# Hybrid decoder trunk: the first quarter of the modulation in two eighths, part of it multiplied by TensorE, and four pieces of the input projection on the first eighth

## The chip, the cores and the metric

The kernel runs on one core of a Trainium2 chip. The metric is the device time of one execution in microseconds (us). Engines: PE = TensorE (matmul; PEld is its weight load), DVE = VectorE, ACT = ScalarE, POOL = GpSimd, SP = SyncE, whose queue issues almost every DMA.

## The reference

Two layers on x of 256 x 2048, all in float32. Each layer first needs its modulation:

```
c_act = silu(c)                                   # 2048
mod = c_act @ ada_w[layer] + ada_b[layer]         # 2048 x 12288 weights per layer
sh_m, sc_m, g_m, sh_f, sc_f, g_f = split(mod, 6)
h = rmsnorm(x, norm_mix[layer]) * (1 + sc_m) + sh_m
mix = attention and gated unit (layer 0) or short convolution (layer 1) of h @ w_in
x = x + g_m * mix
h = rmsnorm(x, norm_ffn[layer]) * (1 + sc_f) + sh_f
x = x + g_f * swiglu(h, ...)
```

w_in of layer 0 is 2048 x 5632: queries, keys, values and the two inputs of the gating unit, 11 groups of 512 columns. Nothing of h exists until the shift (sh_m) and the scale (sc_m) of its features do, so the first matmul of the projection depends on the modulation weights.

## The kernel before, in words

All weights are streamed once from HBM. A piece is 256 rows (two k-tiles of 128) x 512 columns, 512 KB; SP loads it into one of eight `raw` slots, ACT rounds it to its high part `whi` (six slots), DVE subtracts to get the low part `wlo` (in place), and PE multiplies: for each k-tile and each of the two token tiles t three matmuls of 512 columns (high x high, high x low, low x high; L1419 to L1421), 12 matmuls a piece. Two pieces are a unit. `lo_piece`/`hi_piece` work two units ahead of PE (`hi_next`, `lo_next`).

The modulation is a product of one row and a matrix. It is done by DVE: `ada_op(a)` takes one slot of `ada` (128 rows of one k-tile x 1024 columns, 512 KB, six slots) and adds it, times a column of `cact`, to `acc` (L989, L993). After 16 such ops a tile of 1024 columns is summed over k-tiles but not over partitions; `reduce_cols` has PE do that with a moving operand of one column of ones (L1474), eight calls, and `keep_cols` and `quarter_gain` on DVE give `mod` and `gsc`. The tile for the first quarter holds the shift and the scale of features 0 to 511. The order of the modulation tiles is `ADA`, the pace of the ops behind the front is `ADA_PACE`.

The first quarter of h is two tiles (t = 0, 1) of four blocks of 128 features. ACT normalises x (`norm_xn`), PE turns it (`norm_turn`, L1511), ACT scales and shifts it (`norm_scaled`, L669), rounds the high part (`norm_front` for blocks 0 and 1, L680, `norm_back` for blocks 2 and 3, L690), DVE subtracts for the low part (L1055).

The input projection visits its groups by quarters of the features (`VISITS`): first all 11 groups with the first quarter (units 0 to 10), then eight of them with the second, and so on. What a visit leaves in PSUM is evicted by ACT into `kept` (L623); a later visit of the same group begins with ACT writing it back into PSUM (`seed`, L629). PSUM has two accumulators per token tile, used in turn (`acc_bank`), so visit v can begin only when visit v-2 is evicted.

The order of every engine is written out by hand. In the front, PE's program is: idle matmuls on ones (`idle_work`, L1496) paced by DVE's ops 7 to 10 and 12 to 14, a turn, `reduce_cols(0)`, a turn, four idle matmuls, and then the units. SP's program is the column of c, six modulation loads, x, ten modulation loads, four pieces, and then per unit two pieces and the modulation loads of its pace. A modulation load waits until DVE has used the op that had its slot (`summed`). DRAM holds the weights as the reference has them, so that a piece has rows of 2 KB.

Of the kernel before, what the change touches and what calls it, by code (L numbers as in the profile page):

```python
# [14 lines left out]
P = 128  # L15
D = 2048
# [37 lines left out]
VISITS = ([(c, (0,)) for c in IN_ORDER]  # L54
          + [(c, (k,)) for k in (1, 2, 3) for c in IN_ORDER[:EARLY]]
          + [(c, (1, 2, 3)) for c in IN_ORDER[EARLY:]])
IN_UNITS = [(v, c, k) for v, (c, ks) in enumerate(VISITS) for k in ks]
LAST = {c: v for v, (c, ks) in enumerate(VISITS)}
UNIT_OF = {v: max(u for u, x in enumerate(IN_UNITS) if x[0] == v) for v in range(len(VISITS))}
VISIT_AT = {u: v for v, u in UNIT_OF.items()}  # L60
BEFORE = {v: w for v, (c, ks) in enumerate(VISITS) for w in range(v) if VISITS[w][0] == c}

SEEDED = [v for v in BEFORE if len(VISITS[v][1]) == 1]
KEPT = {c: n for n, c in enumerate((0, 3, 1, 4, 2, 5, 9, 10))}
FIRST_OF = {k: min(u for u, x in enumerate(IN_UNITS) if x[2] == k) for k in range(4)}
# [9 lines left out]
GROUP_UNITS = ([len(ks) for c, ks in VISITS] + 4 * [4] + len(F_UNITS) * [1] + (12 - 2 * F_VISITED) * [4] + 4 * [6]  # L75
# [5 lines left out]
GROUP_END = [sum(GROUP_UNITS[:g + 1]) - 1 for g in range(len(GROUP_UNITS))]  # L81
# [8 lines left out]
CLOSING = {2 * u + 1: g for g, u in enumerate(GROUP_END)}  # L90
# [32 lines left out]
ADA = ([(0, SH_M, q) for q in range(4)] + [(0, G_M, n) for n in range(2)]  # L123
       + [(0, SH_F, q) for q in range(4)] + [(0, G_F, n) for n in range(2)]
       + [(1, w, n) for w in (SC_M, SH_M, SC_F, G_M, SH_F, G_F) for n in range(2)])
QUARTERS = 4
QUARTER_OF = {j: (k, q) for k, w in ((0, SH_M), (1, SH_F)) for q in range(4) for j in (ADA.index((0, w, q)),)}
GATES = ((0, G_M), (0, G_F), (1, G_M), (1, G_F))

OPS = [(j, k) for j in range(len(ADA)) for k in range(KT)]  # L130

ANGLES_AT, TRIG_AT = 3, 5
REDUCE_AT = {9: 1, 17: 2, 25: 3}

# [24 lines left out]
def norm_gain(k, q):  # L159
    return 8 + 2 * (k - 2) + q // 2 + 1 if k > 1 else 4 * k + q + 1  # L160
# [29 lines left out]
for j in range(QUARTERS, len(ADA)):  # L190
    u = next(u for u in range(U_END) if ada_to(u) > OPS.index((j, KT - 1))) + 2
    free = [v for v in range(u, U_END) if v - 4 not in SCORE_UNIT and v not in BOUNDARY and not (is_row(j) and v - 4 in BOUNDARY)]
    ADA_REDUCE[j] = tuple(free[:halves(j)])
# [27 lines left out]
for _k in range(4):  # L221
    for _i in range(8):
        BY_SA[_k, _i] = max(BY_SA.values(), default=0) + (2 if (_k, _i) in SHARED else 4)

# [38 lines left out]
def decoder_kernel(nc, x_in, c_col, pos, ada_w, ada_b, g_mix, g_ffn, w_in, sgu_w, sgu_b, w_out,  # L263
                   conv_in, conv_w, conv_out, ff_gate, ff_up, ff_down, g_fin, freq_in, ident_in,
                   mask_in, out):
    with ExitStack() as ctx:
# [94 lines left out]
        ada_step, ada_init, red_done, mod_done, row_done = sems("ada_step ada_init red_done mod_done row_done")  # L361
# [27 lines left out]
        def summed(engine, a):  # L389

            j, k = OPS[a]
            engine.wait_ge(ada_step, KT * j + k + 1)

        def scaled(engine, k, i, blocks=4):
# [5 lines left out]
            else:  # L400
                engine.wait_ge(hf_ready, BY_SA[k, i] - 4 + blocks)
# [9 lines left out]
        def columns_of(v, j):  # L411

            layer, which, n = ADA[j]
            return v[:, :].rearrange("p (w f) -> p w f", f=KT)[:, which:which + 2, 4 * n:4 * n + 4]
# [27 lines left out]
        def rows(w):  # L442
            return w.rearrange("(t p) n -> p t n", p=P)

        def layer_rows(w):
            return w.rearrange("l (t p) n -> l p t n", p=P)

        ada_v, gate_v, up_v, down_v = (layer_rows(w) for w in (ada_w, ff_gate, ff_up, ff_down))
        w_in_v, w_out_v, conv_in_v, conv_out_v = (rows(w) for w in (w_in, w_out, conv_in, conv_out))

        def piece_of(v, k, n):
            return v[:, 2 * k:2 * k + 2, COLS * n:COLS * n + COLS]
# [7 lines left out]
        def feed_pieces(layer):  # L460
            if layer == 0:
                for k, c, w in F_UNITS:
                    for half in range(2):
                        yield piece_of((gate_v, up_v)[w][layer], 2 * k + half, c)
            for half in HALVES:
                for c in half:
                    if visited(layer, c):
                        continue
                    for v, k in in_turn((gate_v, up_v), layer and c == 0):
                        for p in range(2):  # L470
                            yield piece_of(v[layer], 2 * k + p, c)
                for n in range(4):
                    for k in range(2 * half[0], 2 * half[-1] + 2):
                        yield piece_of(down_v[layer], k, n)

        def weight_pieces():

            for v, c, k in IN_UNITS:
                for half in range(2):
                    yield piece_of(w_in_v, 2 * k + half, c)  # L480
            for n, k in OUT_UNITS:
                for half in range(2):
                    yield piece_of(w_out_v, 2 * k + half, n)
            yield from feed_pieces(0)
            for i in range(4):
                for n, k in in_turn((4 + i, 8 + i), i == 0) + [(i, k) for k in range(4)]:
                    for half in range(2):
                        yield piece_of(conv_in_v, 2 * k + half, n)
            for n in range(4):
                for k in range(8):  # L490
                    yield piece_of(conv_out_v, k, n)
# [6 lines left out]
        def _(sp):  # L498
# [7 lines left out]
            def load_ada(a):  # L506
                j, k = OPS[a]
                layer, which, n = ADA[j]
                if a >= ADA_SLOTS:
                    summed(sp, a - ADA_SLOTS)  # L510
                to, w = ada[:, a % ADA_SLOTS], ada_v[layer, :, k, :]
                if j in QUARTER_OF:
                    to = to.rearrange("p (w n) -> p w n", w=2)
                    src = w.rearrange("p (w n) -> p w n", w=6)[:, which:which + 2, COLS * n:COLS * n + COLS]
                else:
                    col = D * which + ADA_COLS * n
                    src = w[:, col:col + ADA_COLS]
                sp.dma_start(to, src).then_inc(ada_loaded[a % ADA_SLOTS], 16)
# [1276 lines left out]
```

## Time and profile before

| | before |
|---|---|
| time, median of 3 runs | 2264.3 us (2264.23 to 2264.5) |
| the profiled execution | 2265.22 us, span 2263.5 us |
| PE busy | 2226.7 us, 98% |
| DVE busy | 1625.4 us, 72% |
| ACT busy | 1154.2 us, 51% |
| DMA queue of SP | 613.5 MB, 80.8% of 16 engines' span |

Busy time is what an engine spent in instructions; the span runs from the first to the last instruction. Times in rows are microseconds from the start of the span. The granted clock is TensorE's, 1.00 for 2.4 GHz and 0.50 for 1.2 GHz.

### The profile page before, as it was taken

To read this page: it belongs to the slowest core of one execution; us is meant where nothing else is said; L and a number is where in the kernel's file an instruction comes from. 1 tells how busy PE (TensorE), PEld (TensorE's weight loads), DVE (VectorE), ACT (ScalarE), POOL (GpSimd) and SP (SyncE) were. 2 spreads that over 40 slices of the span, in tenths; PEclk is the share of its full clock that TensorE was granted. 3 is DMA by queue.
4 is the path that set the end of the run, shared out by engine and by line. 5 is a ranking of instruction groups with operands and counts; after the bars stand their busy time and mean duration, and the time that the engine had idled before them with its cause. 6 is when DMAs were issued, how large, how long until landed. Compare 5 with 4: busy or idle time off the path is not lost.

```text
span 2263.5 us, 26805 instructions
## 1 busy us (share of the span) xinstructions
PE 2226.7 (98%) x10133; PEld 1845.0 (82%) x10133; DVE 1625.4 (72%) x1644; ACT 1154.2 (51%) x1541; POOL 102.6 (5%) x71
## 2 busy tenths in 40 slices
PE   5999999999999999999999999999999999999998
PEld 3888888888888888888888888888888888888887
DVE  6888899788887767777778877887664454545455
ACT  4688774687544344444474444446444433344443
POOL 0003201000000100000100000010000010000010
PEclk9999999999999999999999999999999999999999
DMA  9999889899888888888878888878876666666664
GB/s 346 361 365 353 271 278 342 289 366 323 306 312 284 293 292 289 288 280 288 288 240 306 302 311 307 303 273 278 272 221 191 190 192 189 196 186 194 187 193 141
DMA packets 286033, 615.91 MB, mean 272 GB/s; under 512 B 19792, under 2 KB 20176, under 8 KB 285520
## 3 DMA queue, kind: packets, MB, share of 16 engines
q1 hardware_dynamic: 284464, 613.50, 80.8%
q8 instruction: 81, 1.33, 0.2%
q10 hardware_dynamic: 1440, 0.69, 0.1%
q14 instruction: 48, 0.39, 0.0%
HBM read 612.02 MB, written 2.10 MB: 271 GB/s over the span
## 4 chain that ended last, share of the span: by engine, by line
PE 98%; DVE 1%; DMA 1%; issue 0%; ACT 0%; ACTq 0%; SPq 0%; DVEq 0%
PE ps L1419 31%; PE ps L1421 31%; PE ps L1420 31%; PE ps L1511 3%; DMA ada<-ada_w 1%; PE ps L1474 1%; DVE acc L993 1%; PE ps L1652 0%; PE ps L1601 0%; PE ps L1489 0%; PE ps L1490 0%; PE ps L1651 0%; PE ps L1603 0%; DVE hf L1073 0%; PE ps L1671 0%
## 5 line engine op out<-in xcount | busy, mean ns | idle before, releaser
L965 DVE TENSOR_TENSOR wlo<-raw,whi 128x1024 fp32r<-128x1024 f32 x776 | 938.4, 1236 | 291.2 <-ACT whi L595 289.6
L595 ACT ACTIVATE whi<-raw 128x1024 fp32r<-128x1024 f32 x776 | 805.6, 1058 | 610.4 <-PE ps L1421 431.5
L1419 PE MATMUL ps<-whi,h 128*128 128x512 f32 x2144 | 842.1, 393 | 1.7 <-DVE h L1055 0.9
L1421 PE MATMUL ps<-whi,h 128*128 128x512 f32 x2144 | 835.8, 390 | 0.0
L1420 PE MATMUL ps<-wlo,h 128*128 128x512 f32 x2144 | 835.3, 390 | 0.0
L993 DVE SCALAR_TENSOR_TENSOR acc<-ada,cact,acc 128x1024 f32<-128x1024 f32 x368 | 483.5, 1314 | 21.2 <-DMA ada<-ada_w 9.0
L1419 PEld LDWEIGHTS ps<-whi,h 128*128 128x128 f32 x2144 | 403.0, 188 | 87.1 <-issue 4.9
L1421 PEld LDWEIGHTS ps<-whi,h 128*128 128x128 f32 x2144 | 402.8, 188 | 84.9
L1420 PEld LDWEIGHTS ps<-wlo,h 128*128 128x128 f32 x2144 | 403.2, 188 | 81.9
L1419 PE MATMUL ps<-whi,act 128*128 128x512 f32 x704 | 274.7, 390 | 0.0
L1421 PE MATMUL ps<-whi,act 128*128 128x512 f32 x704 | 274.0, 389 | 0.0
L1420 PE MATMUL ps<-wlo,act 128*128 128x512 f32 x704 | 273.9, 389 | 0.0
L568 POOL TENSOR_TENSOR x<-x,tmp 128x512 f32<-128x512 f32 x40 | 70.0, 1753 | 1908.0 <-DVE tmp L1128 1907.9
L1421 PEld LDWEIGHTS ps<-whi,act 128*128 128x128 f32 x704 | 132.2, 188 | 27.4
L1419 PEld LDWEIGHTS ps<-whi,act 128*128 128x128 f32 x704 | 132.2, 188 | 27.2
L1420 PEld LDWEIGHTS ps<-wlo,act 128*128 128x128 f32 x704 | 132.2, 188 | 27.2
L1419 PE MATMUL ps<-whi,mixed 128*128 128x512 f32 x256 | 100.8, 394 | 0.0
L1421 PE MATMUL ps<-whi,mixed 128*128 128x512 f32 x256 | 99.8, 390 | 0.0
L1420 PE MATMUL ps<-wlo,mixed 128*128 128x512 f32 x256 | 99.7, 389 | 0.0
L1128 DVE TENSOR_TENSOR tmp<-ps,grow 128x512 f32<-128x512 f32 x48 | 33.0, 690 | 86.3 <-PE ps L1421 86.3
L1170 DVE TENSOR_TENSOR prod<-ps,silu 128x512 f32<-128x512 f32 x44 | 29.9, 690 | 81.0 <-PE ps L1421 81.0
L623 ACT ACTIVATE silu<-ps 128x512 f32<-128x512 f32 x44 | 26.2, 599 | 107.4 <-PE ps L1421 107.3
(136 smaller groups left out, 985.5 us busy)
## 6 DMA issues: line engine op xcount, KB each, us to landing
ada<-ada_w SPq DMA_DIRECT2D x384, 512.0 KB, 6.7
raw<-ff_gate SPq DMA_DIRECT2D x176, 512.0 KB, 4.6
raw<-ff_up SPq DMA_DIRECT2D x176, 512.0 KB, 4.6
raw<-ff_down SPq DMA_DIRECT2D x176, 512.0 KB, 4.6
raw<-conv_in SPq DMA_DIRECT2D x96, 512.0 KB, 4.9
raw<-w_in SPq DMA_DIRECT2D x88, 512.0 KB, 5.6
raw<-w_out SPq DMA_DIRECT2D x32, 512.0 KB, 6.3
raw<-conv_out SPq DMA_DIRECT2D x32, 512.0 KB, 5.7
```

The lines of the kernel that those rows point to most:

```text
L568: nc.gpsimd.tensor_tensor(xs, xs, tmp[:, r % 2, :], ALU.add).then_inc(x_pool, 1)
L595: nc.scalar.activation(whi[v % HIGH][:, :, :], raw[:, v % RAW], ACT.Copy).then_inc(hi_ready, 1)
L623: nc.scalar.activation(dst, ps[:, acc_bank(g, t), :], func).then_inc(acc_free[acc_bank(g, t)], 1)
L965: nc.vector.tensor_tensor(wlo[:, v % RAW], raw[:, v % RAW], whi[v % HIGH][:, :, :].bitcast(F32), ALU.subtract).then_inc(lo_ready, 1)
L993: nc.vector.scalar_tensor_tensor(out=to, in0=src, scalar=c, in1=to, op0=ALU.mult, op1=ALU.add)\
L1128: nc.vector.tensor_tensor(tmp[:, r % 2, :], ps[:, acc_bank(g, t), :], grow[:, COLS * n:COLS * n + COLS], ALU.mult).then_inc(acc_free[acc_b ...
L1170: nc.vector.tensor_tensor(prod[:, t, :], ps[:, acc_bank(g, t), :], silu[:, t, :], ALU.mult).then_inc(acc_free[acc_bank(g, t)], 1)
L1419: nc.tensor.matmul(to, high, whi[v % HIGH][:, k, :], start=begin, stop=False, skip_group_check=on)
L1420: nc.tensor.matmul(to, high, wlo[:, v % RAW, k, :], start=False, stop=False, skip_group_check=on)
L1421: ins = nc.tensor.matmul(to, low, whi[v % HIGH][:, k, :], start=False, stop=end, skip_group_check=on)
L1474: ins = nc.tensor.matmul(ps[:, ADA_BANK, COLS - 8 + n:COLS - 7 + n], sums[:, P * n:P * n + P], ones_r[:, 0:1].bitcast(F32), start=True, st ...
L1511: return nc.tensor.transpose(to, src, ident[:, :])
```

## The change

The first quarter of the modulation (features 0 to 511) is cut into two eighths of 256 features. Each has eight loads: a load holds two k-tiles of 128 rows for 512 columns (shift and scale of 256 features). Of the sixteen loads, number 1, 3, 5, 7, 13, 14 and 15 (`BY_PE`) are not added by DVE but multiplied by PE (`eighth_product`: eight calls with the load's 128 x 128 blocks as weights and a column of `cact` as moving operand), in the same PSUM columns in which `reduce_cols` sums what DVE has added of the others (`eighth_op`, two additions of 512 columns a load).

With the first eighth the front half of the first quarter of h is made, and four pieces of the projection (256 rows each, groups 0, 3, 6 and 1) are multiplied with it. Then comes the second eighth, then the back half of h, and the other pieces of these groups. Groups 0 and 3 are visited twice in the first quarter, with a seed between; the pieces of groups 6 and 1 stay in PSUM over the second eighth.

SP's order changes: three modulation loads, x, five, four pieces, seven modulation loads, a piece, the last of the sixteen. A load's slot is free when DVE or PE has read it (`slot_read`). The host now lays out the weights by pieces and by modulation loads, each one block of 512 KB with 4 KB a partition; before, this was a view on the array. No group of the projection and no other stage does other arithmetic than before.

```diff
+EIGHTHS = IN_ORDER[:2]
+VISITS = ([(c, (0,)) for c in EIGHTHS] + [(c, (0, 1)) for c in IN_ORDER[2:4]] + [(c, (1,)) for c in EIGHTHS]
+          + [(c, (0, 1)) for c in IN_ORDER[4:]]
+          + [(c, (2 * k, 2 * k + 1)) for k in (1, 2, 3) for c in IN_ORDER[:EARLY]]
+          + [(c, tuple(range(2, 8))) for c in IN_ORDER[EARLY:]])
+IN_PIECES = [(v, c, p) for v, (c, ps) in enumerate(VISITS) for p in ps]
+IN_PIECES[3], IN_PIECES[4] = IN_PIECES[4], IN_PIECES[3]
+BY_PIECES = 4
+AHEAD = 5
...
+BY_PE = (1, 3, 5, 7, 13, 14, 15)
+LAST_SUM = [6, 12] + LAST_OP[2:]
...
+        def slot_read(engine, a):
+            if a in (7, 15):
+                engine.wait_ge(red_done, a // 8 + 1)
+            elif a in BY_PE:
+                engine.wait_ge(ada_multiplied, sum(b not in (7, 15) for b in BY_PE if b <= a))
+            else:
+                summed(engine, a)
...
@@ SP
             sp.dma_start(cact[:, :], c_col).then_inc(c_loaded, 16)
-            for a in range(ADA_SLOTS):
+            for a in range(3):
                 load_ada(a)
             sp.dma_start(x[:, :, :], x_in.rearrange("(t p) d -> p t d", p=P)).then_inc(x_loaded, 16)
-            for a in range(ADA_SLOTS, KT):
+            for a in range(3, KT // 2):
                 load_ada(a)
-            for v in range(4):
+            for v in range(AHEAD - 1):
                 load_piece(v)
+            for a in range(KT // 2, KT - 1):
+                load_ada(a)
+            load_piece(AHEAD - 1)
+            load_ada(KT - 1)
...
@@ ACT
             hi_piece(0)
+            norm_front(0, 0, 0, SH_M)
+            norm_front(0, 1, 0, SH_M)
             hi_piece(1)
-            norm_quarter(0)
             hi_piece(2)
             hi_piece(3)
+            for v in range(2):
+                for t in range(2):
+                    keep_visit(v, t)
+            hi_piece(AHEAD - 1)
+            norm_quarter(0)
...
@@ DVE
-            for a in range(KT):
-                if a == 12:
-                    for t in range(2):
-                        mean(0, t)
-                    for t in range(2):
-                        inverse(0, t)
-                ada_op(a)
+            for a in (0, 2, 4, 6):
+                eighth_op(a)
+            for t in range(2):
+                mean(0, t)
+            for t in range(2):
+                inverse(0, t)
             ve.wait_ge(const_loaded, 16 * N_CONST)
             keep_cols(0)
             quarter_gain(0)
             lo_piece(0)
             norm_front(0, 0, 0, SH_M)
-            lo_piece(1)
             norm_front(0, 1, 0, SH_M)
-            lo_piece(2)
-            lo_piece(3)
+            for v in range(1, 4):
+                lo_piece(v)
+                eighth_op(v + 7)
+            eighth_op(11)
+            eighth_op(12)
+            lo_piece(AHEAD - 1)
+            keep_cols(1)
+            quarter_gain(1)
+            norm_back(0, 0)
+            norm_back(0, 1)
...
@@ PE
+            def eighth_product(a, first=False, last=False):
+                pe.wait_ge(cact_ready, 1)
+                if a // 8:
+                    pe.wait_ge(mod_done, 1)
+                pe.wait_ge(ada_loaded[a % ADA_SLOTS], 16 * (a // ADA_SLOTS + 1))
+                for half in range(2):
+                    k = 2 * (a % 8) + half
+                    for n in range(4):
+                        at = COLS - 4 + n
+                        ins = nc.tensor.matmul(ps[:, ADA_BANK, at:at + 1], ada[:, a % ADA_SLOTS, COLS * half + P * n:COLS * half + P * n + P],
+                                               cact[:, k:k + 1], start=first and half == 0 and n == 0, stop=last and half == 1,
+                                               skip_group_check=True)
+                ins.then_inc(red_done if last else ada_multiplied, 1)
...
+            eighth_product(1, first=True)
+            eighth_product(3)
+            idle_work(4)
+            eighth_product(5)
+            idle_work(4)
+            reduce_cols(0, first=False, last=False)
+            eighth_product(7, last=True)
             pe.wait_ge(pool_const, 2)
             pe.wait_ge(const_loaded, 16 * N_CONST)
-            for k in range(7, 11):
-                summed(pe, OPS.index((0, k)))
-                idle_work(3)
             norm_turn(0, 0)
-            for k in range(12, 15):
-                summed(pe, OPS.index((0, k)))
-                idle_work(3)
-            reduce_cols(0)
             norm_turn(0, 1)
             idle_work(4)
+            for i in range(BY_PIECES):
+                visit_piece(i)
+            eighth_product(13, first=True)
+            eighth_product(14)
+            reduce_cols(1, first=False, last=False)
+            eighth_product(15, last=True)
+            idle_work(4)
...
@@ host
+    def pieces(w):
+        w = w.reshape(*w.shape[:-2], -1, 2, P, w.shape[-1] // COLS, COLS)
+        return np.swapaxes(w, -4, -2)
```

## Rows read from the trace of the kernel before

**Rows 1.** The page, part 1: busy us, share of the span, instructions.

```profile
PE 2226.7 (98%) x10133; PEld 1845.0 (82%) x10133; DVE 1625.4 (72%) x1644; ACT 1154.2 (51%) x1541; POOL 102.6 (5%) x71
```

**Rows 2.** Waits of PE: us in total, times, longest us.

```profile
PE ps L1496 <- DVE acc L993: 25.4, 3, 24.5
```

**Rows 3.** Chain that ended last, first 100 us: start us, us, what.

```profile
36.12 2.48 PE ps L1474 x16
38.60 0.96 PE ps L1511 x4
39.56 1.71 PE ps L1496 x4
41.27 0.45 PE ps L1419
...
97.12 0.87 PE ps L1511 x8
97.99 1.68 PE ps L1474 x16
```

**Rows 4.** Timeline, DVE and ACT: start us, us, engine, line, what.

```profile
13.98 1.28 DVE L993 SCALAR_TENSOR_TENSOR acc<-ada,cact,acc 128x1024 f32<-128x1024 f32 x1 [0.44 <-DMA ada<-ada_w]
20.06 0.63 ACT L635 ACTIVATE junk<-x 128x512 bf16<-128x512 f32 x1 [17.22 <-DMA x<-x_in]
...
21.41 8.43 DVE L993 SCALAR_TENSOR_TENSOR acc<-ada,cact,acc 128x1024 f32<-128x1024 f32 x6 [6.14 <-DMA ada<-ada_w]
```

**Rows 5.** Timeline, PE, the idle matmuls of the front.

```profile
24.53 5.62 PE L1496 MATMUL ps<-ones_r 128*128 128x512 f32 x12 [24.53 <-DVE acc L993]
...
31.86 0.97 PE L1496 MATMUL ps<-ones_r 128*128 128x512 f32 x3
...
34.64 0.96 PE L1496 MATMUL ps<-ones_r 128*128 128x512 f32 x3 [0.42 <-DVE acc L993]
```

**Rows 6.** Windows: length, busy us (instructions) by engine, PEclk, DMA share, GB/s.

```profile
34.00:35.00 1.00, 0.58 (x3) 0.32 (x3) 0.90 (x2) 0.04 (x1) 0.00 (x0) 1.00 1.06 389
37.00:38.00 1.00, 1.00 (x8) 1.00 (x8) 0.00 (x0) 0.37 (x1) 0.00 (x0) 0.65 1.05 387
...
44.00:45.00 1.00, 1.00 (x5) 0.78 (x4) 0.32 (x1) 1.00 (x3) 0.00 (x0) 0.94 1.05 385
```

**Rows 7.** Timeline, PEld, weight loads of the column sums at half clock.

```profile
37.54 0.55 PEld L1474 LDWEIGHTS ps<-ones_r,acc 128*128 128x128 f32 x2
37.76 0.55 PEld L1474 LDWEIGHTS ps<-ones_r,acc 128*128 128x128 f32 x2
```

**Rows 8.** Windows, the last column is GB/s.

```profile
14.00:17.00 3.00, 0.00 (x0) 0.00 (x0) 1.27 (x1) 0.00 (x0) 0.00 (x0) 1.00 1.03 418
21.40:41.00 19.60, 14.03 (x49) 9.59 (x50) 15.31 (x18) 12.11 (x27) 0.41 (x1) 0.91 1.05 387
```

**Rows 9.** Timeline, from the sum over partitions to the first projection matmul.

```profile
38.71 0.17 DVE L1011 TENSOR_TENSOR mod<-ps,adab 128x8 f32<-128x8 f32 x1 [2.73 <-PE ps L1474]
...
39.16 0.81 ACT L669 ACTIVATE hf<-ps,mod,gsc 128x128 f32<-128x128 f32 x2 [1.79 <-DVE gsc L1035]
...
41.06 0.66 PE L1419 MATMUL ps<-whi,h 128*128 128x512 f32 x1
```

**Rows 10.** Timeline, ACT: after the front, and an eviction with its seed.

```profile
43.76 1.32 ACT L656 ACTIVATE xn<-x,rstd 128x512 f32<-128x512 f32 x2
44.99 2.94 ACT L595 ACTIVATE whi<-raw 128x1024 fp32r<-128x1024 f32 x3
...
94.43 0.60 ACT L623 ACTIVATE kept<-ps 128x512 f32<-128x512 f32 x1 [1.17 <-PE ps L1421]
95.12 0.60 ACT L629 ACTIVATE ps<-kept 128x512 f32<-128x512 f32 x1
95.66 1.05 ACT L595 ACTIVATE whi<-raw 128x1024 fp32r<-128x1024 f32 x1
```

**Rows 11.** Windows, columns as in rows 6.

```profile
44.10:100.00 55.90, 55.90 (x260) 46.69 (x259) 47.72 (x54) 36.59 (x51) 0.00 (x0) 1.00 1.00 357
```

More of the change, by code:

```diff
@@ L88 @@
 GROUP_END[G_CI], GROUP_END[G_F1] = U_CI + 6, U_F1 + 6
-CLOSING = {2 * u + 1: g for g, u in enumerate(GROUP_END)}
+CLOSING = {LAST_PIECE.get(g, 2 * u + 1): g for g, u in enumerate(GROUP_END)}
 USED_TO = [0]
@@ L439, in freed @@
             engine.wait_ge(acc_free[acc_bank(g, t)], g // 2 + 1)
[L442 to L449, printed above, removed]
         def piece_of(v, k, n):
-            return v[:, 2 * k:2 * k + 2, COLS * n:COLS * n + COLS]
+            return v[k, n]
         def in_turn(groups, turns):
@@ L468, in feed_pieces @@
                         continue
-                    for v, k in in_turn((gate_v, up_v), layer and c == 0):
+                    for v, k in in_turn((ff_gate, ff_up), layer and c == 0):
                         for p in range(2):
@@ L1266, in _ @@
                 lo_next(n, 0)
-                if VISIT_AT.get(n) in BEFORE and VISIT_AT[n] not in SEEDED:
-                    add_visit(VISIT_AT[n])
+                for v in VISITS_AT.get(n, ()):
+                    if v in BEFORE and v not in SEEDED:
+                        add_visit(v)
                 lo_next(n, 1)
@@ L1407, in half_unit, with piece @@
             def half_unit(u, g, t, first, last, of, k0, half):
-                v = 2 * u + half
+                piece(2 * u + half, g, t, first and half == 0, last and half == 1, of, k0 + 2 * half)
+            def piece(v, g, t, first, last, of, k0):
                 on = g in SEEDED
@@ L1414, in half_unit @@
                 for k in range(2):
-                    high = of[:, k0 + 2 * half + k, P * t:P * t + P]
-                    low = of[:, k0 + 2 * half + k, S + P * t:S + P * t + P]
-                    begin = first and half == 0 and k == 0
-                    end = last and half == 1 and k == 1
+                    high = of[:, k0 + k, P * t:P * t + P]
+                    low = of[:, k0 + k, S + P * t:S + P * t + P]
+                    begin = first and k == 0
+                    end = last and k == 1
                     nc.tensor.matmul(to, high, whi[v % HIGH][:, k, :], start=begin, stop=False, skip_group_check=on)
@@ L1421, in half_unit @@
                     ins = nc.tensor.matmul(to, low, whi[v % HIGH][:, k, :], start=False, stop=end, skip_group_check=on)
-                if last and half == 1:
+                if last:
                     ins.then_inc(acc_done[t], 1)
@@ L1468, in ready_sums, with reduce_cols @@
                 return acc[:, j % 2, :]
-            def reduce_cols(j):
+            def reduce_cols(j, first=True, last=True):
                 pe.wait_ge(ones_ready, 1)
                 sums = ready_sums(j, 0)
-                for n in range(8):
-                    ins = nc.tensor.matmul(ps[:, ADA_BANK, COLS - 8 + n:COLS - 7 + n], sums[:, P * n:P * n + P],
-                                           ones_r[:, 0:1].bitcast(F32), start=True, stop=True)
-                ins.then_inc(red_done, 1)
+                cols = 2 * blocks_of(j)
+                for n in range(cols):
+                    at = COLS - cols + n
+                    ins = nc.tensor.matmul(ps[:, ADA_BANK, at:at + 1], sums[:, P * n:P * n + P],
+                                           ones_r[:, 0:1].bitcast(F32), start=first, stop=last, skip_group_check=not first)
+                if last:
+                    ins.then_inc(red_done, 1)
+            def eighth_product(a, first=False, last=False):
[3 more added lines that the diff above has]
+                pe.wait_ge(ada_loaded[a % ADA_SLOTS], 16 * (a // ADA_SLOTS + 1))
+                for half in range(2):
+                    k = 2 * (a % 8) + half
[5 more added lines that the diff above has]
+                ins.then_inc(red_done if last else ada_multiplied, 1)
             def turn_cols(j, n):
@@ L1631, in _ @@
                     norm_turn(0, 2 * REDUCE_AT[n] + 1)
-                    reduce_cols(REDUCE_AT[n])
+                    reduce_cols(REDUCE_AT[n] + 1)
                 for b in QK_AT[n]:
@@ L1762, in columns, with modulation @@
         return np.moveaxis(v.reshape(*v.shape[:-1], -1, P), -1, 0)
+    def pieces(w):
+        w = w.reshape(*w.shape[:-2], -1, 2, P, w.shape[-1] // COLS, COLS)
+        return np.swapaxes(w, -4, -2)
+    def modulation(layer, which, n):
+        w = a["ada_w"][layer]
+        if (layer, which) == (0, SH_M) and n < 0:
+            first = 2 * P * (n + 2)
+            w = w.reshape(KT // 2, 2, P, 6, D)[:, :, :, which:which + 2, first:first + 2 * P]
+            return np.swapaxes(w, 1, 2).reshape(KT // 2, P, ADA_COLS)
+        w = w.reshape(KT, P, 6, D)
+        if (layer, which) in ((0, SH_M), (0, SH_F)):
+            return w[:, :, which:which + 2, COLS * n:COLS * n + COLS].reshape(KT, P, ADA_COLS)
+        return w[:, :, which, ADA_COLS * n:ADA_COLS * n + ADA_COLS]
     arrays = {
@@ L1767 @@
         "pos": a["positions"][0].reshape(2, P).T,
-        "ada_w": a["ada_w"],
+        "ada_w": np.concatenate([modulation(*tile) for tile in ADA]),
         "ada_b": columns(a["ada_b"]).reshape(P, -1),
```

183 lines of the change are left out of this document (107 added, 76 removed).

## Prediction

> **What bounds the kernel now.** I read the busy shares first. TensorE (PE) is busy for 2226.7 us of the 2263.5 [rows 1], so only what moves the end of PE's work can move the time. Then PE's waits: nearly all of its idle time is 25.4 us at the front, 24.5 of it before its first matmul, for the modulation sums of VectorE (DVE) [rows 2]. From the first group of the input projection on, the chain that ended last is PE alone [rows 3]. So two things count: when the projection starts, at 41.27 us, and what is put between its matmuls. Ten units of it (24 matmuls each) end at 97.12 [rows 3]. Their first 2.9 us ran at half clock and lost half of that, 1.45; the rest gives 5.44 us a unit, 2.72 a piece of 12 matmuls, 0.227 a matmul. The ninth piece (unit 4) therefore starts at 97.12 - 6 x 5.44 = 64.5 us. I carry the change through to that same piece; behind it both kernels issue the same matmuls.
>
> The front before: six modulation loads have landed by about 14.0, x at 20.06, the seventh load at 21.41 [rows 4]. DVE then adds the last ten at 1.40 us each, PE sums over partitions from 36.12, and the projection starts 2.7 us after that sum [rows 3].
>
> **Prices.** PE's clock decides them. The first dense matmuls began at 24.53, twelve in 5.62 us, at half clock; those of 31.86 ran at full clock [rows 5]. The granted clock was 1.00 in us 34, 0.65 in us 37 and 0.94 in us 44 [rows 6]: it fell in the middle of the sixteen one-column instructions of L1474, 1.7 us after the last dense matmuls (34.64 to 35.60 [rows 5]), and was back some 4.6 us after dense work had started again at 39.56. One column costs a weight load: at full clock sixteen take 1.68 us (0.11 each; a call in the code is two), at half clock they follow each other every 0.21 us [rows 3, 7]. So an `eighth_product` (8 calls, 16 instructions) costs 1.8 us at 2.4 GHz and 3.4 us at 1.2 GHz, `reduce_cols` with 4 columns 0.9 or 1.7. Four idle matmuls at half clock are 1.71 us, four transposes 0.96 [rows 3].
>
> **First eighth (front).** Eight loads instead of sixteen are needed, but x is moved ahead of loads 3 to 7. By bytes, load 3 then lands where the eighth half-megabyte did: halfway between 13.98 and 20.06, at 17.0 us. The host now lays every load out as one block with 4 KB rows. The stretch in which x's 8 KB rows moved had 418 GB/s, that of the 2 KB rows 387 [rows 8]; I take 0.5 us for that and put load 3 at 16.5 (ends 15.5 and 17.0). PE's order behind it is written out: product 3, four idle matmuls, product 5, four idle, `reduce_cols`, product 7. PE has done nothing dense before, so all of it is at half clock: 3.4 + 1.7 + 3.4 + 1.7 + 1.7 + 3.4 = 15.4, which ends at 31.9. The loads (the eighth at about 22) and DVE (four ops, the last at about 23) are done long before: PE has become the bound of the front. The statistics of x hide there too: its eight squares take 6 us from about 15, and the first normalised tile is there before 25. Then two turns and four idle matmuls, 3.6: piece 0 starts at 35.5, 5.8 us earlier than before. Dense work began at 33.8, so full clock is back at about 39 (4.6 to 6 us later, as before). Piece 0 loses 1.6 us where before lost 1.45: +0.15.
>
> **Four pieces ahead.** Pieces 1 to 3 need DVE's low parts, which alternate with the second eighth's additions (each now two of 512 columns, estimate 1.65 us), and ScalarE's (ACT's) eviction of the first groups: the last low part is ready by about 43.5, before PE asks at 45.4. PE ends piece 3 at 39.9 + 3 x 2.72 = 48.1. On SP's queue load 9 waits for product 3, load 11 for product 5, load 13 for product 7 (31.9) and load 15 for DVE's op 9 (about 42), each with what stands behind it, piece 4 and piece 5 among that; at 1.35 us a load the last lands at about 45, before its product. POOL has nothing in this stretch.
>
> **Second eighth (middle).** Nothing hides these: products 13 and 14, a reduction, product 15, 28 calls or 56 instructions, in line between piece 3 and piece 4, where PE multiplied on before. All at full clock 6.2 us; falling after 1.7 us, as before, 10.4. The 2.5 us of turns and sums at 97 us stayed high [rows 3], so I take 4 us high and 20 instructions low: 8.3 us, to 56.4. Then the new wait: modulation, gain, scaling, high part, low part, first matmul, 38.60 to 41.06 before [rows 3, 9]: 2.46 us with only four idle matmuls in it. Piece 4 starts at 58.8. Behind the waiting piece stand all of PE's work and the pieces' slots, so everything later moves with it. Before, this chain was paid once; now once in front and once here.
>
> **Restart.** Behind the same wait ACT has queued, in order: two back halves (1.15 us each), two xn (1.23 together), high parts 5 to 8 (0.95 each), two pairs of eviction and seed (0.69 + 0.54), high part 9, two more pairs, high part 10 and the eviction that lets piece 8 begin [rows 9, 10]. From the first scaling, 1.9 us before piece 4, that is 2.3 + 1.23 + 3.8 + 2.46 + 0.95 + 2.46 + 0.95 + 0.6 = 14.75: piece 8 can't start sooner than 12.85 us after piece 4, where four pieces take 10.9. With the clock low for another 4.6 us it is 13.1. So +2.2 us.
>
> **Sum.** -5.8 (start) + 0.15 + 8.3 (products) + 2.46 (wait) + 2.2 (restart) = +7.3; piece 8 at 71.8 instead of 64.5. DVE then owes 16 more ops before unit 9 asks for the second quarter: by my count it has them within a microsecond of that, 0 to +1. Later loads have the same rate of use and start from a fuller buffer, and the row layout of all later weights is worth nothing, since PE does not wait for them. Ends of the terms: load 3 -1.0/+0.5, products -2.1/+2.1, restart -0.25/+1.0, DVE 0/+1: +4 to +12. The profiled execution was 2265.2 (1.7 us outside the span), the median of the runs 2264.3; a difference applies to either: 2264.3 + 7.3 = 2271.6.
>
> **Rivals.**
> A. *The clock rises in the front.* PE is never idle from 16.5 on; if that brings full clock at about 22, product 5 takes 1.8, idle 0.9, reduction 0.9, product 7 1.8: done at 27.0, piece 0 at 29.5 and at full speed. Piece 3 ends at 40.3, products 6.2 to 8.3, wait 2.46, restart 12.85: piece 8 at 61.9 to 64.0, faster by 0.5 to 2.6 us, 2262.7. It decides from product 5 on. Against it: from 37.3 to 40.7 PE was busy throughout with a like mixture (L1474, turns, idle matmuls) and did not get its clock back [rows 3, 6].
> B. *One-column work holds the clock once it is high.* The front is as I say, products 13 to 15 run at full clock and the restart is quick: 7.3 - 2.1 - 0.25 = +5, 2269.3. For it the stretch at 98 us, against it the fall at 37.3.
> C. *DVE becomes the bound.* Against PE it takes up the second quarter's sums 4 to 5 us later than before; if they miss unit 9, PE idles there and its clock falls: +3 on top, 2275. Against: DVE was idle for 8 of 56 us of that stretch [rows 11].
> D. *Longer rows make the loads so fast that they matter*, 1.6 us by the seventh load. PE hides that in my case; on top of A it gives 2261.1.
> E. *A weight load takes 0.11 us at either clock.* Then the front is bound by the loads and DVE (product 7 ends near 26) and the middle costs 6.2: 6 + 2.1 less than my sum, -0.8, 2263.5. The 0.21 us pitch at half clock speaks against it [rows 7]. The Trainium skill, "TensorE: Matmul & The Clock Gate", section "LDWEIGHTS (loading the stationary operand)", has this rule: 128 columns over 1.2, or 107 ns, with no word of the clock; the trace agrees at full clock and has twice as much at half clock.
>
> **Chances.** My case 0.30, B 0.11, C 0.09: slower by over 4.5 us (0.2%, about what a measurement of this kernel tells from no change). A 0.24, A with D 0.04, E 0.03 and cases in between (full clock for product 7 only) 0.11 are no change. A with D and a middle that ACT and the clock let through without a stall, or a start earlier than I see, 0.08. So slower 0.50, same 0.42, faster 0.08. Range for 8 in 10: from A's 2261.5 to C's 2275.5; the likeliest case by itself is 2268.5 to 2276.
>
> **What would show it.** Right: granted clock 0.50 from 17 to about 39; product 7 ending near 32, 10 us after its load; the first projection matmul near 35.5; about 8 us of one-column instructions from 48; a gap of 0.7 us and then piece 4 near 59; piece 8 near 72. Wrong: clock 1.00 before 25 us and the first projection matmul before 31; products of 1.8 us at half clock; piece 5 following piece 4 at full clock without a wait for ACT; or a gap at or behind unit 9 that before did not have.

## The result and the profile after

The changed kernel takes 2270.4 us (median of 11 runs; 2270.3 without two runs of 3241 and 11592 us, which the ratio leaves out), the kernel before 2264.35 on the same chip: 1.0025 times as long, interval 1.0017 to 1.0034. The prediction was 2271.6. The profiled execution took 2270.29 us with a span of 2268.6; the span of before was 2263.5. The span difference is 5.1 us and that of the medians 6.1, because the profiled execution of before lay 0.9 us above its median, the one of after 0.1 below.

The page after, part 1, against [rows 1]: PE has 20 us more busy time and 103 more instructions, but only 5 us of that lengthen the span, since much of the front's PE work stands where PE idled before.

```profile
PE 2246.7 (99%) x10236; PEld 1866.1 (82%) x10236; DVE 1617.1 (71%) x1648; ACT 1157.5 (51%) x1549; POOL 102.6 (5%) x71
```

The waits of PE after (line waited for, releaser: us in total, times, longest). The 25.4 us for VectorE of [rows 2] are 11.3 for the loads:

```profile
PE ps L1546 <- DMA ada<-ada_w: 11.3, 2, 6.8
PE ps L1475 <- DVE h L1097: 1.3, 4, 0.3
```

The chain that ended last, after (start us, us, what), against [rows 3]. L1546 is `eighth_product`, L1569 the idle matmuls, L1532 the sum over partitions, L1584 the turns, L1475 to L1477 the projection:

```profile
3.13 11.57 DMA ada<-ada_w
14.83 3.54 PE ps L1546 x16
18.37 1.92 PE ps L1569 x4
20.29 3.21 PE ps L1546 x16
23.49 1.92 PE ps L1569 x4
25.41 1.50 PE ps L1532 x8
26.91 3.41 PE ps L1546 x16
30.32 1.81 PE ps L1584 x8
32.13 1.71 PE ps L1569 x4
...
45.28 3.57 PE ps L1546 x32
48.84 1.71 PE ps L1532 x8
50.55 3.43 PE ps L1546 x16
...
58.07 3.80 ACT whi L612 x4
...
102.15 0.87 PE ps L1584 x8
```

Load 3 lands at 14.83, and from there PE has no gap until 53.9. Unit 9 ends at 102.15, 5.03 later than the 97.12 of [rows 3]: the whole difference of the spans has arisen by then.

The windows of after (length; busy us of PE, PEld, DVE, ACT, POOL; PEclk; DMA share; GB/s) for the front, the products at high and at low clock, the first dense matmuls behind them, and the way to unit 9:

```profile
17.00:32.00 15.00, 15.00 (x64) 14.23 (x65) 4.04 (x10) 7.51 (x15) 0.63 (x1) 1.00 1.03 406
...
45.30:48.66 3.36, 3.36 (x31) 3.36 (x32) 1.40 (x2) 0.00 (x0) 0.00 (x0) 0.98 1.01 405
48.66:53.90 5.24, 5.24 (x26) 5.24 (x26) 0.00 (x0) 0.00 (x0) 0.00 (x0) 0.50 1.03 417
56.20:58.90 2.70, 2.68 (x7) 2.16 (x8) 0.42 (x1) 2.67 (x5) 0.00 (x0) 0.53 1.03 410
58.90:102.10 43.20, 42.85 (x188) 34.70 (x187) 41.89 (x46) 32.47 (x48) 0.00 (x0) 1.00 0.89 332
```

PEclk of the first row says 1.00 although the instructions run at half rate (sixteen one-column instructions in 3.2 to 3.5 us; 1.7 us at full clock in [rows 3]). Up to the first recorded change of the clock the column can't be trusted, so for the front I go by durations. From us 35.0 on, 1.2 us after the projection's start, its matmuls follow each other every 0.23 us; 3.2 us into the products (at 48.5) the column falls to 0.50, the lower of the two levels (1.2 GHz). ScalarE (from 42.9) and VectorE (from 46.7) are idle until 54: they wait for the second modulation.

The timeline around the second modulation and the restart, after (start us, us, engine, line; idle time before it and its releaser in brackets), against [rows 9, 10]:

```profile
...
54.00 0.16 DVE L1053 TENSOR_TENSOR mod<-ps,adab 128x4 f32<-128x4 f32 x1 [7.30 <-PE ps L1546]
54.45 0.81 ACT L689 ACTIVATE hf<-ps,mod,gsc 128x128 f32<-128x128 f32 x2 [11.51 <-DVE gsc L1077]
...
56.22 0.79 PE L1475 MATMUL ps<-whi,h 128*128 128x512 f32 x1 [0.34 <-DVE h L1097]
...
66.46 0.50 PE L1475 MATMUL ps<-whi,h 128*128 128x512 f32 x1 [0.35 <-ACT ps L646]
...
69.33 0.39 PE L1475 MATMUL ps<-whi,h 128*128 128x512 f32 x1
```

Piece 4 starts at 56.22, piece 7 at 66.46, after a wait for ScalarE's seed, piece 8 at 69.33: 13.1 us for four pieces that take 10.9 at full clock.

### The profile page after: what moved, and what is told of

Its sections match the earlier page's. It is cut to its first block, busy times and chain, and to the rows that moved or that the text cites. A ratio compares the mean times of both kernels' runs of the same rounds, so it can differ in the third digit from the quotient of the medians.

```text
span 2268.6 us, 27023 instructions
## 1 busy us (share of the span) xinstructions
PE 2246.7 (99%) x10236; PEld 1866.1 (82%) x10236; DVE 1617.1 (71%) x1648; ACT 1157.5 (51%) x1549; POOL 102.6 (5%) x71
## 4 chain that ended last, share of the span: by engine, by line
PE 98%; ACT 1%; DMA 1%; DVE 0%; issue 0%; SPq 0%; ACTq 0%
PE ps L1475 31%; PE ps L1477 31%; PE ps L1476 31%; PE ps L1584 3%; PE ps L1546 1%; PE ps L1532 1%; DMA ada<-ada_w 1%; PE ps L1569 0%; PE ps L1749 0%; PE ps L1674 0%; ACT whi L612 0%; PE ps L1562 0%; PE ps L1563 0%; PE ps L1748 0%; PE ps L1676 0%
## 5 line engine op out<-in xcount | busy, mean ns | idle before, releaser
L1475 PE MATMUL ps<-whi,h 128*128 128x512 f32 x2144 | 842.6, 393 | 2.4 <-DVE h L1097 1.3
L1477 PE MATMUL ps<-whi,h 128*128 128x512 f32 x2144 | 835.9, 390 | 0.0
L1475 PEld LDWEIGHTS ps<-whi,h 128*128 128x128 f32 x2144 | 403.2, 188 | 89.1 <-issue 4.9
L1477 PEld LDWEIGHTS ps<-whi,h 128*128 128x128 f32 x2144 | 402.8, 188 | 85.1
L1022 DVE SCALAR_TENSOR_TENSOR acc<-ada,cact,acc 128x1024 f32<-128x1024 f32 x353 | 464.2, 1315 | 11.3 <-DVE acc L1018 0.5
L1475 PE MATMUL ps<-whi,act 128*128 128x512 f32 x704 | 274.7, 390 | 0.0
L1477 PE MATMUL ps<-whi,act 128*128 128x512 f32 x704 | 274.0, 389 | 0.0
L1477 PEld LDWEIGHTS ps<-whi,act 128*128 128x128 f32 x704 | 132.1, 188 | 27.6
L1475 PEld LDWEIGHTS ps<-whi,act 128*128 128x128 f32 x704 | 132.2, 188 | 27.3
L1475 PE MATMUL ps<-whi,mixed 128*128 128x512 f32 x256 | 100.8, 394 | 0.0
L1477 PE MATMUL ps<-whi,mixed 128*128 128x512 f32 x256 | 99.8, 390 | 0.0
```

The costliest lines, as they stand in the source:

```text
L1022: nc.vector.scalar_tensor_tensor(out=to, in0=src, scalar=c, in1=to, op0=ALU.mult, op1=ALU.add)\
L1475: nc.tensor.matmul(to, high, whi[v % HIGH][:, k, :], start=begin, stop=False, skip_group_check=on)
L1477: ins = nc.tensor.matmul(to, low, whi[v % HIGH][:, k, :], start=False, stop=end, skip_group_check=on)
```

## The experiments

Each was timed with the kernel before on the same chip (2264.35 to 2264.52); ratios are to it. The changed kernel itself was timed only in the measurement above, so differences to its 2270.4 go across measurements. The interval of a ratio is about 2 us to either side; a smaller difference between two kernels is shown only where the traces show it too. The theory throughout is the prediction's: at half clock the one-column instructions bound the front, and in the middle products, chain and restart stand in line.

**Long rows.** `e1_rows_2kb` is the changed kernel with every weight read as before, in rows of 2 KB; the work is the same.

```diff
-            return v[k, n]
+            return v[:, 2 * k:2 * k + 2, COLS * n:COLS * n + COLS]
...
-        "ada_w": np.concatenate([modulation(*tile) for tile in ADA]),
+        "ada_w": a["ada_w"],
```

> The changed kernel with all weights in rows of 2 KB, as before the change. In the traces x landed at 13.3 us and load 3 at 14.8, earlier than bytes at the old rate give (17.0). Theory 1 (rows are worth something only in the front, where TensorE waits for load 3): load 3 comes 1 to 2 us later and the time is 2271.4 to 2272.4, 1 to 2 us above the changed kernel's 2270.4. Rival (rows worth nothing anywhere; x came early only because it was moved ahead): 2270.4. Rival (rows matter through the whole kernel): over 2273.

Measured: 2270.65, ratio 1.0027 [1.0017, 1.0037], neither theory's 1 to 2 us. The rate from us 17 to 32 is 385 GB/s here and 406 in the changed kernel, but load 3 came at 15.09 instead of 14.83, and the kernels below, all with the new layout, have it (or, where VectorE takes it, its addition) between 14.49 and 15.59. So the difference in load 3 is within the scatter: in this kernel the layout is worth no more than 0.2 or 0.3 us, which is not told from nothing, and load 3 at 14.83 instead of my 16.5 is not its doing.

`e2_blocks_only` is the opposite: the kernel before with that layout alone.

```diff
-            return v[:, 2 * k:2 * k + 2, COLS * n:COLS * n + COLS]
+            return v[k, n]
```

> The kernel before with nothing but the block layout of the weights (4 KB a partition). Theory 1: its front is bound by 16 loads and VectorE's additions; loads a few per cent faster let the additions, which run back to back from 21.4 us, start up to 1.5 us earlier: 2262.8 to 2264.3. Rival (layout worth nothing): 2264.35. Rival (layout matters in the whole kernel): under 2262.

Measured: 2262.82, ratio 0.9992 [0.9983, 1.0000]. Its window over the stretch of the second row of [rows 8], where 387 GB/s were moved:

```profile
21.40:41.00 19.60, 13.07 (x55) 9.11 (x55) 14.78 (x20) 11.77 (x25) 1.55 (x1) 1.00 1.03 408
```

408 GB/s, and 1.7 us less than the kernel before on the same chip, with an interval that just reaches 1. PE in that execution:

```profile
34.53 1.92 PE L1461 MATMUL ps<-ones_r,acc 128*128 128x1 f32 x16 [0.52 <-DVE acc L980]
...
38.77 0.50 PE L1406 MATMUL ps<-whi,h 128*128 128x512 f32 x1 [0.91 <-DVE h L1042]
```

The sum over partitions starts at 34.53 instead of 36.12 [rows 3]: 1.6 us by the loads in this one execution, rival D's size, in a front whose sixteen loads are on the path. The rest of the profiled difference (the modulation at 36.55 instead of 38.71 [rows 9], unit 9 ending 2.7 us earlier) goes with the clock, which in this execution did not fall in the sum and was high from the first projection matmul on. How often it does so in either kernel is not traced, so the loads' share of the 1.7 us in the medians is not separated.

**Is PE the bound of the front?** `e3_no_idle` leaves out the eight idle matmuls between the products.

```diff
             eighth_product(3)
-            idle_work(4)
             eighth_product(5)
-            idle_work(4)
             reduce_cols(0, first=False, last=False)
```

> The changed kernel without the two groups of four idle matmuls behind products 3 and 5. Theory 1 (TensorE at half clock is the bound of the front): product 7 ends 3.4 us earlier, the first piece starts near 30.2 instead of 33.6, and the time is 2267.0 (2266.8 to 2268, the higher end if full clock comes back later in piece 0). Rival (the loads or VectorE bound the front): 2270.4, the gap is taken by waits for loads.

Measured: 2266.93, ratio 1.0010 [1.0001, 1.0019], 3.5 us less than the changed kernel; their cost on its chain is 1.92 + 1.92. Its chain:

```profile
14.64 6.96 PE ps L1546 x32
21.60 1.71 PE ps L1532 x8
23.30 3.41 PE ps L1546 x16
...
30.23 0.43 PE ps L1475
```

The projection starts at 30.23 instead of 33.83. Nothing of another engine takes their place: the front is PE's alone.

**Does the clock set the price of a product?** `e4_dense_front` makes PE dense before the first products.

```diff
+            idle_work(18)
             eighth_product(1, first=True)
+            idle_work(8)
             eighth_product(3)
```

> The changed kernel with TensorE kept in dense idle matmuls from 3 us on: 18 of them before product 1, 8 behind it, the rest as it is. Theory 1 (half clock makes the products of the front cost 3.4 us): the granted clock is 1.00 before 10 us, products 3 and 5 take 1.8 us each, the first piece starts at 25.5 to 28 instead of 33.6, and the time is 2262.5 to 2265, that is 5.5 to 8 us less. If the clock falls again among products and short idle work, the lower part of the gain is lost: 2266. Rival (a weight load of one column takes as long at either clock, the products are bound by reading the loads): 2270.4 or more.

Measured: 2268.06, ratio 1.0016 [1.0008, 1.0025], outside both ranges of the theory (2262.5 to 2265, or 2266) and under the rival's. Full clock came, and was lost at the end of product 3. Windows, timeline and chain of this kernel:

```profile
6.70:16.90 10.20, 7.87 (x51) 6.76 (x49) 2.14 (x3) 3.37 (x9) 0.00 (x0) 0.99 1.02 396
16.90:33.90 17.00, 17.00 (x66) 15.51 (x66) 5.76 (x14) 10.99 (x23) 0.63 (x1) 0.51 1.00 394
```

```profile
8.83 1.84 PE L1546 MATMUL ps<-cact,ada 128*128 128x1 f32 x16
...
14.96 2.01 PE L1546 MATMUL ps<-cact,ada 128*128 128x1 f32 x16 [2.33 <-DMA ada<-ada_w]
```

```profile
18.89 3.21 PE ps L1546 x16
...
25.50 3.41 PE ps L1546 x16
```

The same sixteen instructions take 1.84 to 2.0 us at full clock and 3.2 to 3.4 at half. Rival E (0.11 us a weight load at either clock) falls. So does A: from 16.9 to 33.9 PE was busy without a gap, and the clock did not come back among products, short idle work and the sum. That a front which has full clock also loses it by such work alone is not shown, since PE had waited 2.33 us for load 3 just before the fall. Only 1.4 us of start came of it (32.43 instead of 33.83), and the span is 1.5 us shorter.

**Is the chain's wait on the path?** `e5_piece_behind` moves piece 3 behind the second eighth's products, so that PE has it while the modulation is made.

```diff
-            for i in range(BY_PIECES):
+            for i in range(BY_PIECES - 1):
                 visit_piece(i)
             ...
             eighth_product(15, last=True)
-            idle_work(4)
+            visit_piece(BY_PIECES - 1)
```

> The changed kernel with the fourth piece moved behind the products of the second eighth, in place of the four idle matmuls. In the changed kernel product 15 ends at 53.8 us and piece 4 starts at 56.2. Theory 1 (the chain modulation to h is a bare wait, and the one-column work is serial): products end at 51.1, the piece covers the chain, piece 4 starts at about 53.8, and the clock may stay high for more of the products: 2 to 2.5 us less up to piece 4; behind it ACT's queue (12.85 us to piece 8) is what binds, and it too starts 2.7 us earlier. 2267.5 to 2268.4. Rival (loads of the second eighth or VectorE's additions are late there): TensorE waits for load 15 or for the sums, and the time is 2270 or more.

Measured: 2268.36, ratio 1.0015 [1.0006, 1.0023]; the runs lie in two groups, three near 2266.2 and eight at 2268.2 to 2269.6, and the profiled one was of the lower. Its chain:

```profile
45.83 1.02 PE ps L1532 x8
46.85 3.34 PE ps L1546 x16
50.19 0.64 PE ps L1475
```

PE goes from the product into piece 3 at once; the wait of 2.2 us (53.98 to 56.22) is gone, but the first eight matmuls of that piece run at half clock. What separates the two groups of runs I have not traced.

**What do the products of the middle cost against VectorE?** `e6_second_by_dve` gives all eight loads of the second eighth to VectorE.

```diff
-BY_PE = (1, 3, 5, 7, 13, 14, 15)
-LAST_SUM = [6, 12] + LAST_OP[2:]
+BY_PE = (1, 3, 5, 7)
+LAST_SUM = [6, 15] + LAST_OP[2:]
```

> The changed kernel with all eight loads of the second eighth added by VectorE; products 13, 14 and 15 are gone, the rest as it is. VectorE's additions end at 45.6 in the changed kernel; three more take 4.7 us, to 50.3, then the sum over partitions at half clock, 1.7: 52.0 instead of 53.8. Theory 1 (what TensorE spends on products is more than VectorE would need in all): 1.5 to 2 us faster, 2268.5 to 2269, though TensorE now idles 5 us. Rival (the products relieve VectorE, and without them it is the bound): 2271 or more.

Measured: 2268.66, ratio 1.0018 [1.0009, 1.0027]. Its chain has a gap in place of the products:

```profile
46.11 4.93 issue
```

PE is idle for these 4.93 us. The profile names no releaser, but VectorE adds without a gap from 41.20 to 50.9, and PE's sum, which needs these additions, starts at 51.04. Five microseconds of waiting for VectorE's sums stand in place of 7.0 us of products (3.57 + 3.43): 1.75 us are saved in the median, and PE's products are no gain here either.

**Is the restart ScalarE's?** `e8_high_parts_ahead` makes the high and low parts of pieces 5 to 7 before the wait for the second modulation; their slots are free.

```diff
+READY = 8
...
-            hi_piece(AHEAD - 1)
+            for v in range(AHEAD - 1, READY):
+                hi_piece(v)
```

> The changed kernel with the high and low parts of pieces 5, 6 and 7 made before the second eighth's modulation is waited for, where ACT idles from 43 to 54 us, instead of behind the back half of h. Theory 1 (behind the wait ACT's queue is the bound: piece 8 at 12.85 us after piece 4 or later): this queue is 2.8 us shorter, piece 8 comes 10.9 us and the loss at half clock (1.4) after piece 4, 12.3 to 12.5 instead of 13.1: 0.5 to 1 us less, 2269.5 to 2269.9. Rival (clock alone sets the restart): 2270.4. Rival (ACT alone): 2268.2.

Measured: 2269.62, ratio 1.0022 [1.0014, 1.0031]. PE waits for ScalarE no more; the longest of its waits now are

```profile
PE ps L1549 <- DMA ada<-ada_w: 10.9, 2, 6.4
PE ps L1478 <- DVE h L1099: 1.3, 4, 0.3
```

0.8 us is won in the median; in the traces piece 8 starts 11.9 us after piece 4 (55.93 to 67.82) instead of 13.1. Most of the rest of the restart is the clock: in the changed kernel the first six matmuls of piece 4 took 2.64 us (56.22 to 58.86) where full clock needs 6 x 0.227 = 1.36, which is 1.3 us.

**Is VectorE too slow for the front's loads?** `n1_first_by_dve` lets it take all eight; PE runs idle matmuls paced by its sums.

```diff
-BY_PE = (1, 3, 5, 7, 13, 14, 15)
+BY_PE = (13, 14, 15)
...
-            eighth_product(1, first=True)
-            eighth_product(3)
-            ...
-            eighth_product(7, last=True)
+            summed(pe, 2)
+            idle_work(12)
+            for a in range(3, 7):
+                summed(pe, a)
+                idle_work(5)
+            reduce_cols(0)
```

> The changed kernel with all eight loads of the first eighth added by VectorE; TensorE has no products in the front but dense idle matmuls (12 behind load 2, then 5 behind each of loads 3 to 6). VectorE keeps pace with the loads (1.55 us for an addition pair, one load each 1.3 to 1.4): sums done at 22.6, reduction 0.9 to 1.7, first piece at 26.0 to 27.2 instead of 33.6 and at full clock: Theory 1 (TensorE at half clock, not loads nor VectorE, is the bound of the front): 2262 to 2264. Rival (VectorE would be the bound, the products relieve it): not under 2268.

Measured: 2264.16, ratio 0.9998 [0.9989, 1.0007], 6.2 us less than the changed kernel. Its chain:

```profile
22.15 0.76 DVE acc L1039
23.05 1.02 PE ps L1534 x8
...
29.00 0.28 PE ps L1477
```

VectorE has the last sum at 22.9; the changed front had its own at 30.3. The projection starts at 29.0 instead of 33.8, and the span is 4.9 us shorter (this profiled run lay 1.3 us above its median). Four products on PE relieve an engine that was not late. (n1 also has more dense idle matmuls in front; with the products kept, such matmuls alone gave 2.3 us in e4.)

**Products between pieces.** `e10_interleaved` spreads the second eighth's products over pieces 0 to 3.

```diff
-            for i in range(BY_PIECES):
-                visit_piece(i)
-            eighth_product(13, first=True)
-            eighth_product(14)
-            reduce_cols(1, first=False, last=False)
-            eighth_product(15, last=True)
-            idle_work(4)
+            visit_piece(0)
+            visit_piece(1)
+            eighth_product(13, first=True)
+            visit_piece(2)
+            eighth_product(14)
+            reduce_cols(1, first=False, last=False)
+            eighth_product(15, last=True)
+            visit_piece(3)
```

> The changed kernel with the same products, but in another order in the middle: piece 0, piece 1, product 13, piece 2, product 14, reduction, product 15, piece 3. Theory 1 (the middle costs so much because 8.7 us of one-column work stand in one row, in which the clock falls, with a bare wait behind it): the longest such stretch is now 4.5 us at full clock, all products stay at 1.8 us (2.5 to 3 us less), the chain is covered by piece 3 (2.4 less) and piece 4 starts at full clock: 56.2 becomes 50.5 to 51.5. ACT's queue then binds behind it. 2264.5 to 2266. Rival (what the clock loses in the middle is small or falls all the same): 2267.5 to 2268.4, as with the fourth piece moved alone.

Measured: 2265.69, ratio 1.0005 [0.9996, 1.0014]. Its chain:

```profile
39.14 1.68 PE ps L1546 x16
...
43.71 1.68 PE ps L1546 x16
...
46.44 2.50 PE ps L1546 x16
48.94 0.64 PE ps L1475
...
53.85 0.43 PE ps L1477
```

Products 13 and 14 run at 1.68 us, product 15 loses the clock on its way, and piece 3 hides the chain: 4.7 us less than the changed kernel with the same products in another order. The time is in the expected range, but the way there is not as expected: all twelve matmuls of piece 3 run at half clock (48.94 to 54.27, 5.3 us for the usual 2.7), and piece 4 starts at 54.3, not at 50.5 to 51.5. Behind it PE does not wait for ScalarE.

**Together.** `n2_front_dve_behind` is the front of n1 with piece 3 behind and the parts of pieces 5 to 7 ahead (the edits of n1, e5 and e8).

```diff
-BY_PE = (1, 3, 5, 7, 13, 14, 15)
+BY_PE = (13, 14, 15)
+READY = 8
...
-            idle_work(4)
+            visit_piece(BY_PIECES - 1)
```

> Three edits together on the changed kernel: first eighth added by VectorE with dense idle matmuls in front, the fourth piece behind the second eighth's products, and the high and low parts of pieces 5 to 7 ahead. If they add: 2270.4 - 6.2 - 2.1 - 0.8 = 2261.3; with TensorE's clock kept through the products up to 2 us less, 2259.5. Rival (they don't add, since VectorE's additions for the second eighth end at 39.6 and bind): 2263 or more.

Measured: 2261.20, ratio 0.9986 [0.9977, 0.9995]: under both kernels, 3.3 us below before on its chip and 9.2 below the changed one. The three gains add, as expected (2261.3). `n3_front_dve_interleaved` takes the middle of e10 in its place.

```diff
+            visit_piece(0)
+            visit_piece(1)
+            eighth_product(13, first=True)
+            visit_piece(2)
+            ...
```

> As before but with the interleaved middle (piece 0, piece 1, product 13, piece 2, product 14, reduction, product 15, piece 3), the first eighth by VectorE and the high parts ahead. Theory 1: piece 4 at 45 us instead of 56.2, piece 8 at 57 to 58 instead of 69.3: 2258 to 2260, faster than both kernels. Rival (TensorE now waits for the loads or additions of the second eighth): 2261 to 2263.

Measured: 2262.56, ratio 0.9989 [0.9980, 0.9998]: in the rival's range and not in the theory's, though the rival's reason, that PE waits for loads or additions there, is in the trace with 0.3 us only. No better than n2. Its chain, and then the scaling of the second modulation on ScalarE, in n3 and in n2:

```profile
44.23 0.64 PE ps L1480
...
49.56 0.49 PE ps L1480
```

```profile
47.60 0.81 ACT L690 ACTIVATE hf<-ps,mod,gsc 128x128 f32<-128x128 f32 x2 [1.62 <-DVE gsc L1079]
```

```profile
47.56 0.81 ACT L690 ACTIVATE hf<-ps,mod,gsc 128x128 f32<-128x128 f32 x2 [1.62 <-DVE gsc L1079]
```

PE had its sum by 44.2 in n3 and by 44.7 in n2, but the scaling starts at 47.6 in both. The raw pieces of the parts put ahead land late (ScalarE waits for two of them up to 43.6 and 44.9), and VectorE, which makes their low parts first, comes to the modulation only at 47.1. So h is ready for piece 4 at 49.3 in both. PE does not wait for it: all of piece 3 runs at half clock in n3 (44.23 to 49.56), most of it in n2, and piece 4 starts at 49.4 to 49.6 in both. The held modulation and the low clock end together; no run separates which of the two would bind alone.

## Why the prediction was right

The order of events was as forecast, and the sum came out 1.2 us too high against the medians (7.3, measured 6.1), 2.2 too high against the spans. It was no sure forecast: a slower kernel had half of the chances, and the range reached down to 2261.5. Term by term, in the trace of after:

- **Start**: -7.4 (33.83 against 41.27) for -5.8. PE's stretch from load 3 to its turns was 30.32 - 14.83 = 15.5 us for my 15.4. The miss is load 3, at 14.83 and not 16.5. I had put it halfway between the landings of the sixth load and of x [rows 4], as if nothing of x had moved when the sixth load landed. The queues of before say otherwise for the first 14 us (q1 is SP's: packets, MB, share):

```profile
q1 hardware_dynamic: 1867, 3.90, 77.2%
```

  Six loads are 3.15 MB of the 3.90; the other 0.7 MB belongs to what stood behind them, x first. Load 3 of the changed kernel needs four loads and x, 4.2 MB, and before's queue had moved 4.18 MB by 14.8. Bytes over rate would have told me this, the old landings did not. (The changed kernel's queue had moved 4.62 MB when load 3 landed: some of what follows it had moved as well.)
- **Piece 0's clock**: -0.9 for +0.15. Pieces 0 to 3 took 45.28 - 33.83 = 11.45 us, where 4 x 2.72 + 1.45 = 12.3 were needed before. Full clock came 2.9 us after the idle matmuls of 32.13 had begun, and in e3 2.5 us after those of 28.52 (30.98); the 4.6 us that I read from one instance is no constant.
- **Products**: 8.7 (45.28 to 53.98) for 8.3; the clock fell 3.2 us after their start for my 4.
- **Wait**: 2.2 (53.98 to 56.22) for 2.46. e5 took it out, at the price of a piece partly at half clock.
- **Restart**: 13.1 us from piece 4 to piece 8, as forecast (+2.2). Here the size was right and its make-up was not: I had 1.95 for ScalarE's queue and 0.25 for the clock; e8 gives 0.8 for the queue, and 1.3 is the clock. That the term came out is luck.
- **DVE at unit 9**: 0, as forecast: no new gap there or behind.

Sum: -7.4 - 0.9 + 8.7 + 2.2 + 2.2 = +4.8, of the 5.03 us that unit 9 ends later; the last 0.2 is that the timeline, from which the wait and the restart are read, starts a running matmul up to 0.2 us before the chain does. The two larger misses, load 3 and piece 0's clock, both made the forecast too high, so the total did not come out by their cancelling.

Of the rivals, A is refuted by the front's own durations and by e4: PE was busy from 17.0 to 32.0 without a gap and stayed at half clock. B is refuted by the fall at 48.5, C by unit 9, for which PE has no wait on VectorE, E by e4. D was real, but only in the kernel before (e2, a sum 1.6 us earlier); behind a PE-bound front it is too small to be told from the scatter (e1). The Trainium skill, "TensorE: Matmul & The Clock Gate", section "LDWEIGHTS (loading the stationary operand)", gives 107 ns for 128 columns: the full-clock products of `e10_interleaved` (1.68 us for sixteen, 0.105 each) agree, and the trace has twice that at half clock, 3.43 / 16 = 0.21.

So the gain at the front was real, 8.3 us, and the middle took 13.1 us in three ways: for products that PE does in line, for a chain that now is waited for a second time, and for a restart at half clock.

What stays open: the two groups of runs of e5 (in the profiled one full clock came before piece 0, at 33.7), what exactly makes the clock fall and rise within one-column work, and what n2 would give with a modulation whose constants came earlier (in n1 the first modulation began at 24.72 behind them, 0.6 us after its sum over partitions).

## What to carry to other kernels

When a prerequisite is cut in two so that work can start sooner, count the latency chain behind it twice, and keep a piece of ready work to put in each. Before matrix-vector work is moved to the matmul engine, ask what clock it will run at there: here one-column instructions cost 0.105 us each at full clock and 0.21 at half, and behind a stretch of them the dense work started at half clock. And ask whether the engine being relieved was late at all; here VectorE alone had its last sum at 22.9 (n1), when the front with products ended at 30.3.

## What the runs showed of the hardware

- One-column instructions did not hold full clock: it fell 3.2 us into them in the changed kernel (48.5), in product 3 of e4 (16.7, after a wait of 2.33 us), and within product 15 of e10 (47.3), 3.6 us into product 14, the sum and product 15, though dense pieces stand before them. The sixteen of e2 kept it (1.92 us), the sixteen of before did not (2.48 us).
- After such a fall, dense matmuls ran at half clock for a while that differs: 2.6 us from 56.22 in the changed kernel, 5.3 us from 48.94 in e10.
- Groups of four idle matmuls of 512 columns between products did not raise the clock either: 0.51 from 16.9 to 33.9 us in e4, with PE busy throughout.
- Rows of 4 KB instead of 2 KB: 408 against 387 GB/s on this one core (406 against 385 in the changed kernel and e1), with the packets down from 286033 to 170322.
- Transfers queued one behind another overlap: 0.7 MB of what stood behind six loads of 3.15 MB had moved when the last of the six had landed (14.0 us).
